# Feed-forward as Strassen's seven block products, the down projection as a stage of its own, and three mixed tiles split early

## The reference, cut to what matters

```python
h = h + rmsnorm_2(mix, post_mix_norm[i])
hn = rmsnorm_2(h, pre_ffn_norm[i])
ff = (jax.nn.silu(hn @ w_gate[i]) * (hn @ w_up[i])) @ w_down[i]
h = h + rmsnorm_2(ff, post_ffn_norm[i])
e = rmsnorm_2(p[i] @ w_ple_proj[i], ple_norm[i])
gate = jax.nn.sigmoid(h @ w_ple_gate[i] + b_ple_gate[i])
h = h + e * gate
```

## Time and profile before

| | us |
|---|---|
| median of three runs | 2233.96 (2233.95 to 2238.43) |
| the profiled execution's own time | 2236.91 |
| its span, first to last instruction | 2234.9 |
| PE busy | 2070.4 (93% of the span) |
| DVE busy | 1167.0 (52%) |
| ACT busy | 702.9 (31%) |
| POOL busy | 697.1 (31%) |
| mean granted TensorE clock | 0.962 of full |

### The profile page before, as it was taken

The page is one execution under the profiler, slowest core; times in us unless marked ns, Lnnn a source line. Parts: engine busy times, 40 slices in busy tenths (PEclk is TensorE's granted clock), DMA queues, the critical chain, the costliest instruction groups (busy, mean ns, idle before and its releaser), DMA issues.

```text
span 2234.9 us, 24674 instructions
## 1 busy us (share of the span) xinstructions
PE 2070.4 (93%) x9915; PEld 1710.5 (77%) x9915; DVE 1167.0 (52%) x1596; ACT 702.9 (31%) x1222; POOL 697.1 (31%) x454
## 2 busy tenths in 40 slices
PE   5999989998999999978887898999999999999878
PEld 5987757776778888857666677888888888888767
DVE  5253148987776454464555455444444344444735
ACT  4021227876432223245655443100000000000541
POOL 0333218986000000035665000433444333334020
PEclk9999989999999999979999898999999999999989
DMA  3112100000423101100000321111111111111102
GB/s 142 57 38 86 38 1 1 1 1 2 154 81 132 44 33 38 39 29 20 20 10 20 122 85 59 64 48 48 48 48 48 48 56 48 47 48 66 38 29 94
DMA packets 34304, 113.42 MB, mean 51 GB/s; under 512 B 3664, under 2 KB 5456, under 8 KB 34192
## 3 DMA queue, kind: packets, MB, share of 16 engines
q1 hardware_dynamic: 24336, 88.20, 12.0%
q10 hardware_dynamic: 9856, 23.65, 2.8%
HBM read 103.46 MB, written 8.39 MB: 50 GB/s over the span
## 4 chain that ended last, share of the span: by engine, by line
PE 77%; DVE 12%; ACT 4%; POOL 4%; issue 2%; DMA 0%; ACTq 0%; SPq 0%; POOLq 0%; DVEq 0%
PE psb L316 22%; PE psa L316 20%; PE psd L316 10%; PE psc L316 9%; PE psd L936 2%; PE psd L1855 2%; PE psc L914 1%; POOL pb L1073 1%; PE psc L1818 1%; DVE wl L344 1%; DVE tiny L1786 1%; PE psc L357 1%; DVE ptl L1037 1%; DVE tiny L1020 1%; DVE ltl L1839 1%
## 5 line engine op out<-in xcount | busy, mean ns | idle before, releaser
L327 POOL TENSOR_TENSOR wh<-wraw,one 128x1024 fp32r<-128x1024 f32 x78 | 148.8, 1908 | 757.3 <-PE psc L316 319.7
L330 POOL TENSOR_TENSOR wl<-wraw,wh 128x1024 fp32r<-128x1024 f32 x78 | 187.6, 2405 | 6.1
L316 PE MATMUL psb<-mh,wh 128*128 128x512 f32 x512 | 175.1, 398 | 2.4 <-issue 2.4
L316 PE MATMUL psa<-mh,wh 128*128 128x512 f32 x448 | 159.4, 408 | 16.8 <-ACT mh L1116 14.0
L316 PE MATMUL psb<-ml,wh 128*128 128x512 f32 x512 | 173.1, 394 | 0.0
L316 PE MATMUL psb<-mh,wl 128*128 128x512 f32 x512 | 172.9, 393 | 0.0
L316 PE MATMUL psa<-ml,wh 128*128 128x512 f32 x448 | 156.6, 402 | 1.9 <-DVE ml L2132 1.4
L316 PE MATMUL psa<-mh,wl 128*128 128x512 f32 x448 | 155.2, 399 | 0.0
L1073 POOL TENSOR_TENSOR pb<-pb,tiny 128x1024 f32<-128x1024 f32 x64 | 121.3, 1895 | 89.1 <-DVE tiny L1031 87.5
L2181 ACT ACTIVATE th<-hf 128x1024 f32<-128x1024 f32 x22 | 23.3, 1061 | 391.4 <-DVE hf L2195 391.4
L1951 POOL TENSOR_TENSOR qks<-krr,one 32x1024 fp32r<-32x1024 f32 x2 | 5.5, 2756 | 418.0 <-DVE krr L1639 417.9
(11 more groups left out here) (556 smaller groups left out, 5062.4 us busy)
## 6 DMA issues: line engine op xcount, KB each, us to landing
wraw<-slabs SPq DMA_DIRECT2D x160, 512.0 KB, 3.5
x<-xT SPq DMA_DIRECT2D x8, 520.0 KB, 9.4
h<-xT ACTq DMA_DIRECT2D x8, 512.0 KB, 6.5
residual<-h ACTq DMA_DIRECT2D x8, 512.0 KB, 6.2
h<-residual ACTq DMA_DIRECT2D x8, 512.0 KB, 7.1
outT<-h ACTq DMA_DIRECT2D x16, 256.0 KB, 2.0
ct<-dft ACTq DMA_DIRECT2D x1, 1300.0 KB, 5.7
st<-dft ACTq DMA_DIRECT2D x1, 1300.0 KB, 9.9
```

What stands on the lines that cost most here:

```text
L316: t = e.matmul(o, lhsT=lw, rhs=xx(kt, c0, cn), start=n == 0, stop=n == total - 1, skip_group_check=True)
L327: e.tensor_tensor(WH[j][:, :], RAW[:, j, :], ONE[:, 0:1].to_broadcast([P, 1024]), MUL).then_inc(*pooled.up(("high", s)))
L330: e.tensor_tensor(WL[j][:, :], RAW[:, j, :], WH[j][:, :], SUB).then_inc(*pooled.up(("split", s)))
```

## The change

It has four parts.

- **Seven products in place of eight.** A product of 2x2 blocks is made in Strassen's way: seven block products of sums of blocks. For gate and up of a chunk the weight is 2 k halves (j) by 2 output tiles (i), the input 2 k halves by 2 token halves (l). A *unit* is one product of a 512x128 weight block with a 512x512 input block: 12 matmuls. The list `UNITS` holds 10 chunks x 2 weights (w = 0 gate, 1 up) x 7 = 140 units, chunk 1 with gate and up in turns, and then 7 x 11 = 77 units for down (product by product, 11 k tiles each, 4 output tiles at a time). Chunk 0 stays as it was.
- **Operands of the units.** Products 1, 2, 5, 6, 7 take a sum or difference of two weight blocks (POOL, `pool_sum`), 1, 3, 4, 6, 7 one of two input blocks (DVE). POOL now makes all low parts (`pool_low`), ACT all high parts (`act_high`), into eight weight buffers (`WRH`/`WRL`). For gate and up the input sums are made once, at the start, from `H` scaled by ACT in place (`act_scaled_input`), and kept in memory; `H` is first written to DRAM (`residual2`) and reloaded at the end. For down they are made per unit (`dve_b_sum`, `dve_b_low`), with six buffers, three in the last product.
- **Down as one stage.** The hidden tiles go to DRAM (`hidden_dram`, ACT's queue) and come back in blocks `HB`. The down weights come as 132 blocks of 128x512, and products are added into `FA` at each product's end instead of per chunk.
- **Mixed tiles 4, 5, 6 of half 0** are split during the last MLA units, and PE makes their share of the first two quarters (18 matmuls) ahead of the last `pe_mla_out`. The residual's eight loads stand behind the splits.

The diff, cut:

```diff
-_stage(68, 6 * (DFF // 256) - 4)
+S_GATE_UP, S_DOWN = 68, 68 + 4 * (DFF // 256 - 1)
...
+        NW = 8
+        NR = 4
+        WR = at("wr", [P, NR, 1024], F32, 140)
+        _at = (156, 160, 164, 168, 124, 128, 132, 136)
+        WRH = [at(f"wrh{j}", [P, HALF], F32R, _at[j]) for j in range(NW)]
+        WRL = [at(f"wrl{j}", [P, HALF], F32R, _at[j] + 2) for j in range(NW)]
...
+        EARLY, LATE = (4, 5, 6), (0, 1, 2, 3, 7)
+
+        def pe_out2_early(e):
+
+            for n in range(2):
+                e.wait_ge(*acted.on(("mexp", NM2 - 2)))
+                project(e, S_OUT2 + n, [(kt, kt) for kt in EARLY], mh, ml, [(quarter(n), 0, HALF)], ("out2", n),
+                        hi=lambda kt: acted.on(("mix2", "high", kt, 0)), lo=lambda kt: vec.on(("mix2", "low", kt, 0)),
+                        total=3 * KT)
+
...
+            act_split_half(e, MX, 0, "mix2", LATE[:4])
             e.wait_ge(*vec.on(("mout", NM2 - 1)))
+            act_split_half(e, MX, 0, "mix2", LATE[4:])
+            act_split_half(e, MX, 1, "mix2", EARLY + LATE)
             for m in range(KT):
                 load(e, f"h2{m}", H[:, m, :], hs[m])
-            act_split_half(e, MX, 0, "mix2")
...
+        WEIGHTS = {1: ((0, 0), (1, 1), ADD), 2: ((1, 0), (1, 1), ADD), 3: ((0, 0),), 4: ((1, 1),),
+                   5: ((0, 0), (0, 1), ADD), 6: ((0, 0), (1, 0), SUB), 7: ((0, 1), (1, 1), SUB)}
+        TOKENS = {1: ((0, 0), (1, 1), ADD), 2: ((0, 0),), 3: ((0, 1), (1, 1), SUB), 4: ((1, 0), (0, 0), SUB),
+                  5: ((1, 1),), 6: ((0, 0), (0, 1), ADD), 7: ((1, 0), (1, 1), ADD)}
+        UP_ORDER = (2, 1, 5, 7, 6, 3, 4)
+        DOWN_ORDER = (2, 1, 4, 7, 5, 6, 3)
...
+        UNITS = [(1, w, p) for p in UP_ORDER for w in range(2)]
+        for _c in range(2, NCK):
+            UNITS += [(_c, w, p) for w in range(2) for p in UP_ORDER]
+        NUP = len(UNITS)
+        UNITS += [(p, kt) for p in DOWN_ORDER for kt in range(NKT)]
+        NALL = len(UNITS)
+        NDOWN = NALL - NUP
...
+        def pool_sum(e, n):
+            if summed(n):
+                wait_weights(e, n)
+                if n >= NW:
+                    e.wait_ge(*psum.on(("unit", n - NW)))
+                elif n >= 6:
+                    e.wait_ge(*psum.on(("o2 sums", 1)))
+                x, y = weight_blocks(n)
+                e.tensor_tensor(WRF[n % NW][:, :], x, y, WEIGHTS[product(n)][2]).then_inc(*pooled.up(("sum", n)))
+
+        def act_high(e, n):
+            if summed(n):
+                e.wait_ge(*pooled.on(("sum", n)))
+                x = WRF[n % NW][:, :]
+            else:
+                wait_weights(e, n)
+                x = weight_blocks(n)[0]
+            if n >= NW:
+                e.wait_ge(*psum.on(("unit", n - NW)))
+            elif n >= 6:
+                e.wait_ge(*psum.on(("o2 sums", 1)))
+            e.activation(WRH[n % NW][:, :], x, ACT.Copy).then_inc(*acted.up(("high part", n)))
+
+        def pool_low(e, n):
+            e.wait_ge(*acted.on(("high part", n)))
+            x = WRF[n % NW][:, :] if summed(n) else weight_blocks(n)[0]
+            e.tensor_tensor(WRL[n % NW][:, :], x, WRH[n % NW][:, :], SUB).then_inc(*pooled.up(("low", n)))
+
+        def pool_ffn(e):
+            for n in range(NALL + 1):
+                if n < NALL:
+                    pool_sum(e, n)
+                if n >= 1:
+                    pool_low(e, n - 1)
+
+
...
+        def act_scaled_input(e, m):
+            e.wait_ge(*landed[f"spill2{m}"].on("all"))
+            e.wait_ge(*vec.on(("n3 low", m, 1)))
+            e.activation(H[:, m, :], H[:, m, :], ACT.Copy, scale=col("pre_ffn", m)).then_inc(*acted.up(("x", m)))
...
+        def dve_x_lows(e, p):
+            for kt in range(4):
+                high, low, x = x_product(p, kt)
+                e.wait_ge(*acted.on(("x high", p, kt)))
+                e.tensor_tensor(low, x, high, SUB).then_inc(*vec.up(("x low2", p, kt)))
...
+        def pe_up_unit(e, n):
+            c, w, p = UNITS[n]
+            e.wait_ge(*pooled.on(("low", n)))
+            if c == 1:
+                if p in (2, 1):
+                    e.wait_ge(*vec.on(("scaled" if p == 2 else "hidden", 0, w)))
+                if p not in (2, 5):
+                    e.wait_ge(*vec.on(("x low2", p, 3)))
+            elif p == 1:
+                e.wait_ge(*acted.on(("copied", c - 1, w, 7)))
+            elif p in (2, 5, 3):
+                e.wait_ge(*vec.on(("added", c - 1, w, {2: 6, 5: 4, 3: 3}[p])))
+            if p in (7, 6, 4):
+                e.wait_ge(*acted.on(("copied", c, w, {7: 1, 6: 2, 4: 5}[p])))
+            if p == 4:
+                e.wait_ge(*vec.on(("added", c, w, 7)))
+            o = up_bank(w, p)
+            for kt in range(4):
+                high, low, _ = x_product(p, kt)
+                for pas, (wt, x) in enumerate(((WRH, high), (WRH, low), (WRL, high))):
+                    t = e.matmul(o, lhsT=wt[n % NW][:, kt * P:kt * P + P], rhs=x,
+                                 start=kt == 0 and pas == 0 and p not in (7, 6), stop=kt == 3 and pas == 2,
+                                 skip_group_check=True)
+            t.then_inc(*psum.up(("unit", n)))
+
...
+        def act_copied(e, n):
+            c, w, p = UNITS[n]
+            e.wait_ge(*psum.on(("unit", n)))
+            m, l = {2: (1, 0), 1: (1, 1), 5: (0, 1), 7: (0, 0)}[p]
+            if w == 0 and c >= 2:
+                e.wait_ge(*hidden[c % 2][m].on(c - 2) if c > 2 else hidden[0][m].on(0))
+            if w == 1 and c >= 2:
+                e.wait_ge(*vec.on(("hidden", c - 1, m)))
+            e.activation(result(c, w, m, l), up_bank(w, p), ACT.Copy).then_inc(*acted.up(("copied", c, w, p)))
+
...
+        def dve_b_sum(e, i):
+            if two(i):
+                wait_hidden(e, i)
+                wait_slot(e, i)
+                e.tensor_tensor(BLF[slot(i)][:, :], hidden_block(i, 0), hidden_block(i, 1), TOKENS[UNITS[NUP + i][0]][2]
+                                ).then_inc(*vec.up(("b sum", i)))
...
+        def pe_down_unit(e, i):
+            n = NUP + i
+            q, kt = divmod(i, NKT)
+            p = DOWN_ORDER[q]
+            e.wait_ge(*pooled.on(("low", n)))
+            e.wait_ge(*vec.on(("b low", i)))
+            for m in range(4):
+                if kt == 0:
+                    if q < 2:
+                        e.wait_ge(*acted.on(("copied", NCK - 1, q, 7)))
+                        e.wait_ge(*vec.on(("added", NCK - 1, q, 4)))
+                    else:
+                        e.wait_ge(*vec.on(("sum", q - 2, m)))
+                    if q in (2, 4, 6):
+                        e.wait_ge(*acted.on(("taken", q - 2, m)))
+                for pas, (wt, x) in enumerate(((WRH[n % NW], BH), (WRH[n % NW], BL), (WRL[n % NW], BH))):
+                    t = e.matmul(down_bank(q, m), lhsT=wt[:, m * P:m * P + P], rhs=x[slot(i)][:, :],
+                                 start=kt == 0 and pas == 0 and p != 7, stop=kt == NKT - 1 and pas == 2,
+                                 skip_group_check=True)
+            t.then_inc(*psum.up(("unit", n)))
...
+        def act_ffn(e):
+            for m in range(KT):
+                act_scaled_input(e, m)
+            act_x_highs(e, 1)
+            act_high(e, 0)
+            act_high(e, 1)
+            act_tanh(e, 0, 0)
+            for n in range(2, 5):
+                act_high(e, n)
+            act_tanh(e, 0, 1)
+            act_high(e, 5)
+            act_high(e, 6)
+            for n in range(NUP):
+                c, w = n // 14 + 1, n % 14
+                if UNITS[n][2] in (2, 1, 5, 7):
+                    act_copied(e, n)
+                act_high(e, n + 7)
+                if c == 1 and w in (1, 2, 4, 5):
+                    act_x_highs(e, {1: 7, 2: 6, 4: 3, 5: 4}[w])
+                if w == 3 and c != 2:
+                    act_hidden_store(e, c - 1)
+                if c == 1 and w == 13:
+                    act_tanh(e, 1, 0)
+                if c == 2 and w == 2:
+                    act_tanh(e, 1, 1)
+                if c == 2 and w == 5:
+                    act_hidden_store(e, 1)
...
+        def dve_ffn(e):
+            dve_x_sums(e, 1)
+            dve_scaled(e, 0, 0)
+            dve_x_lows(e, 1)
+            dve_gated(e, 0, 0)
+            dve_hidden(e, 0, 0)
+            dve_scaled(e, 0, 1)
+            dve_gated(e, 0, 1)
+            dve_hidden(e, 0, 1)
+            dve_x_sums(e, 7)
+            dve_x_sums(e, 6)
...
+            for i in range(NDOWN):
+                q, kt = divmod(i, NKT)
+                if kt < 4 and q:
+                    dve_sum(e, q - 1, kt)
+                if i + 6 < 6 * NKT:
+                    dve_b_sum(e, i + 6)
+                if i + 5 < 6 * NKT:
+                    dve_b_low(e, i + 5)
+                if 6 * NKT <= i + 3 < NDOWN:
+                    dve_b_sum(e, i + 3)
+                    dve_b_low(e, i + 3)
+                dve_end_early(e, i)
...
+            for m in range(4):
+                dve_sum(e, 6, m)
```

(4 more changed lines are left out.)

635 lines of the change are left out of this document (442 added, 193 removed).

## The result

The changed kernel takes 2213.0 us (median of four runs, 2211.4 to 2214.5), the kernel before beside it 2236.2 (2234.0 to 2240.2). The ratio is 0.9897, with a 95% interval from 0.9884 to 0.9911: 23 us faster, where 49 to 51 were forecast. The profiled execution has a span of 2210.3 us against 2234.9, 24.6 less, and that difference is accounted for here.

The account below looks back on a forecast made before the run. PE was taken as the bound, busy 678.1 of 681.2 us. Terms -84.3 +23 +4 +11 -3 -2 +2 = -49.3 on 2236.9 give 2187.6, or 2184.7 us as a median; range 2155 to 2222.

Parts of the forecast that it names:

- Matmuls: Gate, up and down: 372 fewer matmuls at 0.2267 us each, -84.3 us.
- The price of an operation and of a meeting: POOL and DVE: a POOL operation costs 1.36 us; a 512-column DVE operation between two of POOL's costs POOL 0.33.
- rival 3: POOL and DVE queues simply add, nothing overlaps: down +48, total 2237 us, half-way 2211; chance 0.17.
- The start of gate and up: First units after chunk 0: PE waits 4.9, 3.5 and 7.2 us, plus low clock after each, +23 us.
- Gate and up after that: Later chunks: POOL needs 37.8 us a chunk against PE's 38.1; +4 us for nine, from 0 to 17.
- Down: Down stage: POOL's lead over PE falls short in products 1 and 6, last product 3 us; +11, from 0 to 45.
- no lead: Upper end for down, where POOL has no lead: 29 us, and 16 of loads, 45 in all.
- The mixed tiles: Before gate and up: quarter 2's weights ready at 1256.4 against 1259.5; -3 us, from +1 to -8.
- The end: Norm sums' waits mostly go, -2 us; DVE's additions and sums after the last matmul, +2, from 0 to 8.
- Rival 4: Down: short waits in most units bring PE's lower clock, 5.1 us a unit instead of 2.72; 2257 us; chance 0.07.
- Rival 1: POOL's lead hides nearly all waits: +12, 0, +2 in place of 23, 4, 11; 2161 us; chance 0.16.

Follow-up runs that it names:

- (c): Changed kernel with DVE making the sixth product's input sums behind the seventh's low parts at the start, and ACT rounding the seventh's inputs one step earlier: 2210.6 us.

## Why the prediction was half right

**Matmuls.** Right. 1680 and 924 matmuls at the old spacing of 0.2267 us.

**The price of an operation and of a meeting.** Right, where POOL and DVE both have two. Product 1 in the changed kernel, DVE and POOL:

```profile
1854.19 1.77 DVE L2525 TENSOR_TENSOR blf<-hb,hb 128x512 f32<-128x512 f32 x1
1856.63 1.04 DVE L2539 TENSOR_TENSOR bl<-blf,bh 128x512 fp32r<-128x512 f32 x1 [0.67 <-ACT bh L2534]
1857.59 1.77 DVE L2525 TENSOR_TENSOR blf<-hb,hb 128x512 f32<-128x512 f32 x1
...
1855.38 1.74 POOL L2292 TENSOR_TENSOR wrl<-wrf,wrh 128x512 fp32r<-128x512 f32 x1
1857.08 1.73 POOL L2274 TENSOR_TENSOR wrf<-wr 128x512 f32<-128x512 f32 x1
1858.78 1.75 POOL L2292 TENSOR_TENSOR wrl<-wrf,wrh 128x512 fp32r<-128x512 f32 x1
```

POOL's operations come every 1.70 us (1.69 was worked out from the earlier trace rows) and a unit is 3.40 (3.38). Full locking without the overlap, as in rival 3, would be 1.36 + 0.69 = 2.05 for a pair. The Trainium skill (SBUF - State Buffer, "Who interferes with whom") calls such a meeting an exclusive lock, in which the engine that comes second "fully blocks". The trace agrees, but for the 0.14 us at each start.

**The start of gate and up.** Right by the steps given, and too small: waits of 4.4, 3.4 and 8.5 us for POOL's low part, DVE's scaling and DVE's low parts of the input (4.9, 3.5 and 7.2 worked out), and matmuls at the lower level behind them. Behind the third, from 1442.4 on, the matmuls start 0.43 us apart for some 3 us; behind the waits of the start it is 6 to 10 matmuls each time, where twelve were reckoned. One wait was overlooked, 4.8 us at 1478.4 for a weight's low part, and nearly all of the 30.3 us of gate and up stand before 1485. As (c) shows, moving one of these waits brings out the next. That DVE, ACT and POOL all work off a backlog there, and that the backlog costs the time, would explain it, and isn't shown.

**Gate and up after that.** Right: +4 was forecast, from 0 on. POOL is busy 378.07 of 411.20 us, and PE doesn't wait in chunks 3 to 10.

**Down.** This is the step that failed: +11 against +37.3. The sentence was "in units of lead: product 2 loses 1.3, 1 loses 2.7, 4 wins 5 or fills up, then 7, 5, 6 lose 6.7 together". It has a slip in its own terms: at 2.1 us a unit product 4 wins 2.5 to 3.2 units in its 30 us, not 5, which would have made the term 4 to 6 us larger. That isn't what failed. It counted one lead, POOL's, in front of PE. The late operand was DVE's `bl`, and lead that POOL wins is of no use to DVE. On the contrary: while POOL works ahead, each DVE operation with two SBUF inputs waits for one of POOL's. In down before its last product, DVE's groups, which the earlier trace rows has at 686 ns for the same form without POOL, and POOL's:

```profile
L2539 DVE TENSOR_TENSOR bl<-blf,bh 128x512 fp32r<-128x512 f32 x45 | 68.2, 1519 | 8.5 <-ACT bh L2534 8.4
L2525 DVE TENSOR_TENSOR blf<-hb,hb 128x512 f32<-128x512 f32 x45 | 63.8, 1418 | 0.0
...
L2292 POOL TENSOR_TENSOR wrl<-wrf,wrh 128x512 fp32r<-128x512 f32 x50 | 82.1, 1643 | 1.5 <-ACT wrh L2287 0.8
L2274 POOL TENSOR_TENSOR wrf<-wr 128x512 f32<-128x512 f32 x49 | 80.8, 1650 | 10.1 <-DMA wr<-slabs 10.1
```

Product 4, which was to win 5 units, runs without a wait for seven units. In its last four POOL already makes sums for product 7, DVE has `bl`, `blf` and output sums, and a unit takes 3.2 to 3.4 us, so it lost 2.6 us and left no lead for product 7. The first six products have 24.7 us on top. The forecast's own end of "no lead" (11x3x0.67 + 22x0.33 = 29) is nearer to that than its 8. The price of one meeting had been worked out for POOL (0.33 us) and never for DVE, where it's 0.7 to 1.1. Three runs bear this out: without POOL's sums, without DVE's sums, and with one operation moved from POOL to DVE, which leaves the number of operations as it was (that run has the earlier release too, which the run with the release alone tells apart). In numbers, of the 37.3 us:

- 6.3 to 8.0 come from the late release of the load buffers (half the loads 5.7, earlier release alone 6.3, in another run 8.0). The forecast had it at nothing ("No POOL work waits for it"); it had counted the room between loads and not when the buffer comes free.
- about 17 are the turns of POOL and DVE in the first six products (196.3 or 198.0 with the earlier release, 179.6 with the low parts on DVE).
- 12.6 are the last product, forecast 3. Its three input buffers were seen, and "2.0 us with no waits" was taken for the chain; the loop runs through ACT's order, POOL's operation and DVE's turn, 3.69 us. With DVE late already, 3.0 us of the 12.6 stand before late inputs, 6.9 at the norm sum, and 2.3 in the unit behind it, most of it at the lower clock.

**The mixed tiles.** 3.5 against 3, within a spread of 3: nothing speaks against it.

**The end.** After the last matmul +6.0 against +2; beside the matmuls of the stage -6.6 against -2. DVE's additions and norm sums end at 2072.9, 10 us behind the last matmul, as forecast. The cover of small products wasn't whole. What PE waited for after 2062 us, the two lines that before didn't have or had at 0.2:

```profile
PE psa L339 <- ACT eb L2857: 2.0, 1, 2.0
...
PE psb L339 <- DVE fa L2587: 1.4, 1, 1.4
```

and PE behind the first of them, where two matmuls of a group start 0.85 us after the two before and not 0.46:

```profile
2076.06 0.89 PE L339 MATMUL psa<-ph,wh 128*128 128x512 f32 x2 [2.05 <-ACT eb L2857]
2076.75 1.05 PE L339 MATMUL psa<-pl,wh 128*128 128x512 f32 x2
2077.60 1.05 PE L339 MATMUL psa<-ph,wl 128*128 128x512 f32 x2
```

**The rivals.** Rival 3, that the queues add, was nearest in the time (2211 half-way to it), by luck, as the mechanism was another than it named: POOL isn't slower than forecast. Rival 4 is refuted: with 0.40 to 0.43 us of waiting in unit after unit the first six products show a granted clock of 1.00. The 0.92 of the last product comes from the stretch behind the wait of 4.86 us, where ten matmuls start 0.43 us apart, and costs 2 us. Rival 1 didn't happen: DVE's operations with two SBUF inputs average 1.4 us in down.

**A better kernel.** With the low parts of down's weights on DVE, in the last product between the input's sum and its low part, and with the load buffer released at the sum, it's 2178.8 us, 0.9744 of before (0.9730 to 0.9757), and less than the changed kernel by 34 us. Its down stage, the first two products, then four, then the last:

```profile
1819.25:1849.20 29.95, 29.95 (x132) 24.80 (x133) 28.25 (x28) 12.38 (x23) 17.84 (x12) 1.00 1.00 357
1849.20:1879.10 29.90, 29.90 (x134) 24.75 (x133) 29.90 (x43) 16.15 (x29) 6.40 (x4) 1.00 0.83 302
1879.10:1998.90 119.80, 119.80 (x531) 99.18 (x530) 115.73 (x139) 57.01 (x100) 49.99 (x33) 1.00 0.58 199
1998.90:2033.20 34.30, 33.20 (x146) 27.14 (x145) 24.29 (x37) 14.49 (x22) 0.00 (x0) 0.95 0.23 77
```

PE is busy throughout six products. DVE is nearly full too (115.73 of 119.80), so there is little room to move more to it.

## What to carry to other kernels

Where two engines take turns at a resource, work out the pace of each of them, and keep a lead for each: the time that an engine wins by working ahead can be taken from the one that it makes wait, and the operand that is late may be that one's. Moving an operation of 1.3 us from one of them to the other, where it takes 0.7, can free both. For a stretch with few buffers, follow one buffer around through every engine's order until it comes back to itself; idle time that isn't on this loop was worth nothing here. Then look at what else hangs on the same turn: here a small sum in the same queue held PE longer than the inputs did. And look at what releases a load's buffer before looking at the bandwidth.

## What the runs showed of the hardware

- POOL's 128x512 operation with two SBUF inputs takes 1.28 us undisturbed (2026.65 in the timeline above), and with a DVE operation in turn with it 1.70. DVE's takes 0.68 alone and 1.77 behind a whole POOL operation. With two of each in a unit the pace is 3.36 to 3.45 us a unit, in 27 units of down.
- In the kernel with all low parts on DVE six products ran without a wait of PE, the first of them at 357 GB/s with a DMA share of 1.00; with POOL's sums left out it was 377 GB/s and 1.03. Loads in number held up nothing there.
- Waits of 0.4 us in each unit of 3.4 left the granted clock at 1.00, and so did one of 1.87 us in down's first product. Behind waits of 2.05, 4.86 and 8.52 us matmuls ran at the lower level for some 3 to 4 us; the first two stand next to the eight small matmuls of a norm. Why a wait of 2 us has this effect at one place and not at another, no run here took up.
- The first unit of gate and up came between 1406.6 and 1411.9 us in twelve profiles of the same code up to there, so a difference of 2 or 3 us at one place of two profiles says nothing.
